# A low-rank gate tile projected in four column groups of 32, with its sum taken by the gate product

## The reference, cut to what matters

```
h = rmsnorm(x, g_pre)
(c_x, c_b, c_c, c_z, g_q, g_k, g_v, g_lr, g_z,
 s_q, s_k, s_v, s_z, m_q, m_z) = split_cols(h @ w_in)       # g_lr is 16 columns wide, the others 64 to 256
...
log_a = jax.nn.log_sigmoid((g_lr @ gla_wg + gla_bg).astype(jnp.float32)) / GLA_GATE_NORM
o_b, new_gla = gla_recurrence(g_q, g_k, g_v, log_a, gla_s)
```

## Time and profile before

| | |
|---|---|
| median of 3 runs | 2184.91 us (2183.52 to 2186.13) |
| profiled execution, first to last instruction (its only own time) | 2180.1 us |
| TensorE (PE) busy | 2071.0 us, 95% |
| VectorE (DVE) busy | 1228.0 us, 56% |
| ScalarE (ACT) busy | 855.0 us, 39% |
| GpSimd (POOL) busy | 335.2 us, 15% |
| mean granted TensorE clock | 0.979 of full speed |

### The profile page before, as it was taken

How to read it: one execution, slowest core, us unless ns; L and a number is a source line. 1 busy time by engine, 2 the same in 40 slices (tenths; PEclk the granted TensorE clock), 3 DMA queues, 4 the chain that set the end, 5 groups by cost and what they waited for, 6 DMA issues and landing times. The chain is left out here.

```text
span 2180.1 us, 43454 instructions
## 1 busy us (share of the span) xinstructions
PE 2071.0 (95%) x16698; PEld 1321.2 (61%) x16698; DVE 1228.0 (56%) x2763; ACT 855.0 (39%) x1981; POOL 335.2 (15%) x267
## 2 busy tenths in 40 slices
PE   8999899999999998997999998999999999999898
PEld 4555455568666665666855444455776666656677
DVE  5477665455367754553645775555644776644423
ACT  4554333444354332333435542343435453232311
POOL 1443332000000000000133342320100000000000
PEclk9999999999999999998999998999999999999999
DMA  7431223347410222335353132223561113131532
GB/s 263 128 98 50 75 72 97 97 154 257 118 48 24 65 61 69 85 101 193 127 137 105 62 84 82 83 89 108 188 237 49 60 41 82 35 94 42 159 123 87
DMA packets 196936, 224.92 MB, mean 103 GB/s; under 512 B 53974, under 2 KB 138460, under 8 KB 196700
## 3 DMA queue, kind: packets, MB, share of 16 engines
q1 hardware_dynamic: 193620, 211.55, 31.3%
q10 hardware_dynamic: 3112, 10.59, 1.5%
HBM read 144.98 MB, written 66.10 MB: 97 GB/s over the span
## 5 line engine op out<-in xcount | busy, mean ns | idle before, releaser
L1934 PE MATMUL bank<-h_hi,w_parts 128*128 128x512 f16 (+4 forms) x4240 | 841.1, 344 | 17.5 <-ACTq L2309 9.8
L1934 PEld LDWEIGHTS bank<-h_hi,w_parts 128*128 128x128 f16 (+1 forms) x4240 | 403.2, 98 | 360.4 <-issue 58.0
L1934 PE MATMUL bank<-h_lo,w_parts 128*128 128x512 f16 (+3 forms) x2160 | 441.3, 343 | 3.4 <-DVEq L2560 1.1
L1934 PEld LDWEIGHTS bank<-h_lo,w_parts 128*128 128x128 f16 (+1 forms) x2160 | 205.4, 98 | 176.6 <-issue 18.9
L3011 PE MATMUL bank<-scr_r,tb_r 128*128 128x512 f32 x768 | 192.3, 409 | 21.5 <-DMA scr_r<-w_out_kept 12.4
L3011 PEld LDWEIGHTS bank<-scr_r,tb_r 128*128 128x128 f32 x768 | 149.4, 197 | 56.0 <-issue 13.0
L2308 ACT ACTIVATE tb<-bank 128x512 f32<-128x512 f32 (+1 forms) x140 | 71.3, 509 | 247.8 <-PE bank L1934 227.4
L2841 POOL TENSOR_SCALAR w_raw<-w_raw 128x1024 f32<-128x1024 f32 x46 | 129.6, 2822 | 80.0 <-DMA w_raw<-in_w_in 79.6
L3078 ACT ACTIVATE junk<-bank 128x512 bf16<-128x512 f32 (+1 forms) x68 | 40.6, 597 | 243.7 <-PE bank L3011 233.4
L2441 ACT ACTIVATE scr<-bank,stat 128x256 f32<-128x256 f32 x256 | 117.4, 470 | 34.0 <-DVE stat L2787 31.2
L2461 ACT ACTIVATE scr<-bank 128x1024 f32<-128x1024 f32 x64 | 65.5, 1023 | 163.7 <-PE bank L2205 163.3
(11 more groups left out here) (304 smaller groups left out, 2813.8 us busy)
## 6 DMA issues: line engine op xcount, KB each, us to landing
w_in_kept<-w_parts SPq DMA_DIRECT2D x104, 256.0 KB, 4.3
w_parts<-w_in_kept SPq DMA_DIRECT2D x104, 256.0 KB, 2.9
w_raw<-in_w_in SPq DMA_DIRECT2D x48, 512.0 KB, 4.1
out<-scr SPq DMA_DIRECT2D x32, 512.0 KB, 2.6
scr<-in_x_prompt SPq DMA_DIRECT2D x16, 512.0 KB, 4.3
w_out_kept<-scr_r SPq DMA_DIRECT2D x16, 512.0 KB, 6.3
scr_r<-w_out_kept SPq DMA_DIRECT2D x16, 512.0 KB, 5.9
scr<-out SPq DMA_DIRECT2D x16, 512.0 KB, 4.2
```

The source lines that it names most:

```text
L1934: m = mm(bank[b][0:m_w, 0:c1 - c0], w[:, k, 0:m_w], h[:, k, c0:c1], start=it["piece"] == 0 and k == 0, stop=it["piece"] == 2 and k == KT - 1)
```

## The change

The eight blocks of the `lr` tile go in turn to partitions 0, 32, 64 and 96 of the bank, that is to four groups of 32 columns of TensorE. Each group holds the sum of two blocks, and the four sums are not added in the bank. ACT copies all 128 partitions, and `gate_w` holds the 16 rows of gate weights eight times, so that the gate product adds the parts up. The bias leaves that product. It is held as two columns, `gate_b`, and added where ACT and DVE read the bank. The row of ones goes, and so does its memset. The planner's cost of an `lr` piece of four matmuls becomes that of one matmul.

```diff
         elif k == "proj":
             cols = it["span"]["c1"] - it["span"]["c0"]
-            us = (it["ks"][1] - it["ks"][0]) * (0.004 + cols / 2400)
+            us = (1 if it["role"] == "lr" else it["ks"][1] - it["ks"][0]) * (0.004 + cols / 2400)
...
-    gate_w = sb(ctx, "gate_w", [2 * RANK + 1, GW])
+    gate_w = sb(ctx, "gate_w", [P, GW])
+    gate_b = sb(ctx, "gate_b", [P, 2])
...
-        lr = low[0:2 * RANK + 1]
+        lr = low[:]
...
-            (gate_w[0:RANK, :], of_layer(gla_w_gate, l)),
-            (gate_w[RANK:2 * RANK, :], of_layer(gla_w_gate, l)),
-            (gate_w[2 * RANK:2 * RANK + 1, :], of_layer(gla_b_gate.rearrange("l d -> l () d"), l)),
+            *[(gate_w[o:o + RANK, :], of_layer(gla_w_gate, l)) for o in range(0, P, RANK)],
...
+            params.append((gate_b[:, g:g + 1],
+                           of_layer(gla_b_gate.rearrange("l (g p) -> l g p", g=2)[:, g].rearrange("l p -> l p ()"), l)))
...
                     for k in range(k0, k1):
-                        m = mm(bank[b][0:m_w, 0:c1 - c0], w[:, k, 0:m_w], h[:, k, c0:c1],
-                               start=it["piece"] == 0 and k == 0, stop=it["piece"] == 2 and k == KT - 1)
+
+                        o = 2 * RANK * (k % 4) if lr_here else 0
+                        m = mm(bank[b][o:o + m_w, 0:c1 - c0], w[:, k, 0:m_w], h[:, k, c0:c1],
+                               start=it["piece"] == 0 and k < (4 if lr_here else 1), stop=it["piece"] == 2 and k >= KT - (4 if lr_here else 1))
...
-                        fn(lr[0:2 * RANK, span["c0"]:span["c1"]], bank[b][0:2 * RANK, 0:span["c1"] - span["c0"]], ACT.Copy,
+                        fn(lr[:, span["c0"]:span["c1"]], bank[b][:, 0:span["c1"] - span["c0"]], ACT.Copy,
                            scale=UNSCALE).then_inc(tile_copied, 1)
...
-                    link(fn(la, bank[6][:, 0:n], ACT.Abs))
+                    if not second and it["seq"] == 0:
+                        act.wait_ge(loaded, 16 * len(params))
+                    link(fn(la, bank[6][:, 0:n], ACT.Abs, bias=gate_b[:, s["g"]:s["g"] + 1]))
...
-                    link(ts(gate_area(s, "b"), bank[6][:, 0:width(s)], 0.0, None, ALU.min))
+                    if not second and it["seq"] == 0:
+                        dve.wait_ge(loaded, 16 * len(params))
+                    link(ts(gate_area(s, "b"), bank[6][:, 0:width(s)], gate_b[:, s["g"]:s["g"] + 1], 0.0, ALU.add, ALU.min))
...
-            nc.gpsimd.memset(low[2 * RANK:2 * RANK + 1, :], 1.0).then_inc(ones_done, 1)
```

More of the change, by code:

```diff
@@ L1976, in on_tensor @@
                     pe.wait_ge(tile_copied, copy_no[(lr_step, "lr")])
-                    pe.wait_ge(ones_done, 1)
                     if not second and it["seq"] == 0:
@@ L2820, in on_gpsimd @@
                 link(nc.gpsimd.memset(carry[:], 1.0))
-                link(nc.gpsimd.memset(carry[:, 0:NS:NT], 0.0))
-            nc.gpsimd.memset(low[2 * RANK:2 * RANK + 1, :], 1.0).then_inc(ones_done, 1)
-            pool.wait_ge(ones_done, 1)
+                nc.gpsimd.memset(carry[:, 0:NS:NT], 0.0).then_inc(ones_done, 1)
+                pool.wait_ge(ones_done, 1)
             if not second:
```

## The result

The changed kernel is slower. Its median is 2189.77 us (2184.24 to 2195.49, 20 runs) against 2183.83 us of the kernel before (2178.64 to 2187.92, 20 runs). The ratio is 1.0028, with a 95% interval of 1.002 to 1.0037. The forecast was 2164 us, with a range of 2158 to 2176. The profiled execution took 2184.57 us, its span is 2182.7 us. That is the second shortest of the 20, 5.2 us under their median, so the trace shows less of the loss than the median does. I read the new trace term by term.

A forecast was written before the change was run, and what follows sets the result against it. TensorE, busy 95% of the span, was taken as the bound. Savings of 20.6 us (`lr` tiles) and 4.5 (gate), less 2 for waits and 2 for order, took 2184.9 us to 2164, range 2158 to 2176.

The forecast's parts named there:

- Hidden edits: SP's queue ahead of `w_raw`: added parameter transfers, about 4 us once a layer, hide; otherwise at most 4 us a layer.
- the chain: SP, GpSimd, ACT, GpSimd behind the parameter transfers, making tile 4's low part 17.5 us before TensorE uses it.
- The re-laid order: Planner moves filler behind cheaper `lr` tiles, opening or closing waits: 2 us lost, from 5 gained to 8 lost.
- The last rival: Slower: re-laid filler leaves a hole in unit B, half 0, with a low clock; 2190 us, chance 0.04.
- What is late next: TensorE behind z and `lr` tiles: bank waits give back 2 us, upper end 4; softmax waits about nothing.
- The `lr` tiles: TensorE's narrow low-rank matmuls in four column groups: a 512 tile falls from 3.55 to 1.04 us, saving 20.6 in all.
- The floor of 34 ns a matmul: Instruction floor read from L2164 with 128 columns: sixteen `lr` matmuls take 0.54 us however narrow, a 256 tile 0.6.
- L2164's 3.7: Speedup of 4 in an existing 64-row by 32-column matmul with four column groups, taken for the `lr` tiles.
- the pair's 1.66: Speedup of 2 at L2230's two column groups, the lower end: 11.3 us saved; as rival 2171 us, chance 0.08.
- The gate product: TensorE's gate matmuls with 128 rows instead of 33 lose their extra 0.30 us each: 4.5 us saved, bounds 0 and 6.

The follow-up runs named there:

- e1: The changed kernel with the planner's old cost line, so every engine's order is that of the kernel before: 2182.7 us, ratio 1.0004.
- e4: The changed kernel with the planner's old cost and the parameter transfers behind the store of tile 2: 2165.8 us, ratio 0.992.
- e2: The changed kernel, new order kept, with its parameter transfers issued behind the store of tile 2 instead of ahead of `w_raw`: 2170.78 us, ratio 0.9937.
- f3: The kernel before with seven more transfers, which nothing reads, on SyncE ahead of `w_raw`: 2195.16 us, ratio 1.0058.
- f1: The kernel before with its own 12 parameter transfers moved behind the store of tile 2: 2182.58 us, ratio 0.9995.
- e3: The kernel before with the planner's new cost line alone, so the new order with the old arithmetic: 2193.41 us, ratio 1.0039.
- g3: The changed kernel with transfers behind the store of tile 2 and the new cost in the two first passes alone: 2162.55 us, ratio 0.9899.
- g4: As g3, with tile 0's store ahead of `w_raw` as well: 2158.34 us, ratio 0.9876.
- f2_gate_only: As e4 without the column groups, low-rank blocks written to partitions 0 to 31 again; wrong gate values, for timing only: 2176.15 us, ratio 0.9967.

## Why the prediction was wrong

**The step that failed is that on the parameters, in "Hidden edits": "It hides. If not, it would cost the excess, at most 4 us a layer."** The count of 4 us on SyncE was right (3.8), though by parts that cancel. The eight gate transfers took 5.06 us, 0.63 each and not 0.47, the first bias column took 0.49 and not 0.8, and one `gla_g` that had taken 1.55 us took 0.43. The cover was wrong. I measured it for the last link of the chain, tile 4's low part, which had 17.5 us of lead. The chain passes through ScalarE's in-order queue, and there the copy started 0.19 us behind the instruction before it (ScalarE's rows above), with the exponentials of the next block behind it. In the second layer it already waited 3.14 us for the store. I asked whether the product of the chain is late for its reader. I had to ask what else stands behind each of its links. The store of tile 0 is not in that chain of data at all: it only frees the ring slot, and I did not follow it. The size was off too. Against at most 4 us a layer, 19 transfers ahead cost 17 us in the old order (`e1` less `e4`) and 19 in the new (changed less `e2`), and seven idle ones 12 us (`f3` less `f1`). The wait occurs in the first pass of both layers, and `f3` shows that this alone is enough. Two more things add to it in the changed kernel, in shares that no run gives: TensorE arrives 2.6 us sooner, and the clock falls behind each hole.

**The re-laid order** was priced at 2 us lost, from 5 gained to 8 lost. It costs 5 us with the transfers behind (`e2` less `e4`), 7 us with them ahead (changed less `e1`), and 10 in the old arithmetic (`e3` less the kernel before). So it is a term mis-sized, at the edge of its range or beyond. Where: it loses in the second passes, by 8 us (`e2` less `g3`). In the first passes it puts the copy ahead of the exponentials, and there it gains 3 us with the parameters behind (`e4` less `g3`) and 7.5 with the store first as well (`e4` less `g4`). With the parameters ahead, the long wait eats this gain. The last rival had a hole in unit B as its mechanism. The kernel is slower as in that rival, but the large hole is in unit D of the first passes, where that rival did not look. That its 2190 us is the measured time is luck.

**What is late next** was priced at 2 us for the bank behind a z tile, and at "about nothing" for the scores and transposes. The bank's waits rose by 4.2 us, from 9.8 in the earlier trace rows to 14.0, and stay at 9.8 in the old order. The scores and the softmax are the larger term. In `e4_both` TensorE waits 1.2, 2.0 and 2.0 us at the scores and 3.0 at the transposes behind the `lr` tiles of the four passes, some 8 us. In `f2_gate_only`, where an `lr` tile still takes 3.55 us, the same stretches have none of these. The row of `e4_both` at the first one:

```profile
66.63 1.13 PE L2184 MATMUL bank<-mem_kt,tb 64*128 64x256 f32 x8 [1.25 <-ACTq L2450]
```

The long `lr` tile had been the cover of ScalarE's exponentials. I took the sum of the filler between first scores and transposes, and not what must be done before the second scores.

**The `lr` tiles** were right: 1.04 us forecast for 512 tokens, 0.98 measured. By lines the six of them fell to:

```profile
L1937 PE MATMUL bank<-h_hi,w_parts 128*32 128x512 f16 x48 | 3.7, 383 | 1.2 <-issue 1.2
L1937 PE MATMUL bank<-h_lo,w_parts 128*16 128x512 f16 x48 | 3.7, 379 | 0.0
```

By start times the first eight take 48.41 - 47.98 = 0.43 us, 54 ns each against 215, a ratio of 4.0. The second eight, to the next tile, take 0.55, so a gap of 0.12 stays, where 0.11 was forecast. The floor of 34 ns a matmul, which set the forecast of 0.6 us for a tile of 256 tokens, does not hold here: in `e4_both` its sixteen matmuls take 560.85 - 560.40 = 0.45 us, 28 ns each. L2164's 3.7 was the better guide than the pair's 1.66. The 3.07 of the Trainium skill ("TensorE: Matmul & The Clock Gate", "Measured speedup vs the span model") is for a single pack of four row groups. Here two rounds of four column groups go through in each eight matmuls, at 4.0 times, and the measurement decides. Of the 20.6 us of work that was forecast to go, 10.4 reached the median. TensorE's busy time, which was to fall by 25 us, fell by 18.7 in the changed kernel and by 27.4 in `e4_both` (2043.6 us), so the work did leave. The same arithmetic took longer where more of it ran at the lower clock: the mean granted clock is 0.972 in the one trace and 0.982 in the other.

**The gate product** was right: 4.5 us forecast, the gap of 0.11 ahead of it and the 0.19 within it are gone. 6.4 us, good to 3.5, were measured, for the gate together with the moved bias.

**The account.** From 2183.3 us (the mean of the three medians of before): -0.7 for the transfers behind, -6.4 for the gate, -10.4 for the column groups, +16.9 for the 19 transfers ahead, +7.1 for the order make 2189.8. These are differences of neighbouring kernels, so they add up by construction; each is good to 3 or 4 us. The forecast had -25.1 for the arithmetic and +2 for its waits, where -16.8 came, 0 for the transfers, where it is +16.2, and +2 for the order, where it is +7.1. So of its error of 26 us, 16 are the transfers', 6 the arithmetic's with its waits, and 5 the order's, less 1.6 for the lower start.

**What stays open.** No run separates VectorE's 5.63 us from the wait ahead of it, or prices the lost clock by itself: the 4.5 us behind the two holes are an estimate. Of the 8 us that the new order costs in the second passes, 3.6 are bank waits, and the rest was not traced. Whether the new order gains in the first passes or part of its wait is free is not settled. And 10.4 us by medians against 16.0 by the two profiled spans, for the column groups, is a difference that five timings of each kernel don't settle; the trace of `e4_both` is of its fastest execution, 5.3 us under the median.

## What to carry over

Before an issue of DMAs is called hidden, follow every instruction that waits for what stands behind it in its queue, the reader of the data and also the one that waits for a store to free a buffer. Look at the slack of that instruction in its own engine's queue, and at what stands behind it there. When work is taken out of the busiest engine, what was just in time becomes late, here by up to the 2.6 us that an `lr` tile lost, so list the waits that end within that time of their use. Try small parameter loads behind the big loads and stores of the stage where they are used later: that was worth 17 and 19 us with 19 of them, and nothing with 12 in the kernel before.

## What the runs showed of the hardware

- Four column groups of 32 (128 rows, 512 columns, float16) run at 4.0 times the pace of one after the other, 54 ns a matmul against 215 over eight of them, and 0.12 us are lost at the change back to the full array.
- VectorE's four scalings of 128x256 float32 end within 0.5 us of GpSimd's two-operand instructions: 5.63 us beside two of 4.27 us together, and 5.36 beside 4.28 in `e1_old_order`, against 1.14 alone. The Trainium skill ("SBUF — State Buffer", "Who interferes with whom") says that VectorE in a two-port mode and GpSimd share a port pair that one of them holds for a whole instruction. The trace agrees for GpSimd's TENSOR_TENSOR. It does not for its TENSOR_SCALAR, beside which the same four took 1.37 us. No run shows which mode VectorE was in.
- With 8.7 and 9.6 us of TensorE idle in 20, the granted clock was 0.50 for 10.2 us around and behind each hole, 0.88 and 0.74 as the mean of the 20. TensorE worked for 9.05 of these 20.4 us, so the lower clock cost some 4.5 us (estimate).
- Loads and stores in one SyncE queue were issued 3.75 us later for seven small transfers ahead of them (`f3_seven_more`), and the instruction that waits for the first store started 3.78 us later.
